# A decoder block on one core: wider runs for two scratch tensors in HBM

## The chip, the cores and the metric

One core of one Trainium2 chip. The metric is the device time of the whole program in microseconds (us), median of several executions; lower is better. Before: 1619.41 us, median of 3 runs (1616.14 to 1623.07).

## What is computed

One layer on 512 tokens of width 1024: a state-space mixer and an attention mixer side by side, then a layer of 16384 small experts. Only the expert layer matters here. Cut to that:

```python
def _peer(h, w_query, keys1, keys2, u_tab, v_tab):      # u_tab, v_tab: 16384 x 1024
    ...
    expert = e1 * PEER_NKEYS + e2                        # 8 heads x 16 experts of each token
    g = jax.nn.softmax(top_s.astype(jnp.float32), axis=-1)
    act = jax.nn.gelu(jnp.einsum('thkd,td->thk', u_tab[expert], ht))
    return jnp.einsum('thk,thkd->td', g * act, v_tab[expert])
```

## The kernel before

The expert layer takes two thirds of the time. For 384 of the 512 tokens it is computed densely: the 16384 experts are 128 blocks of 128 (a block is one value of `e1`, its 128 partitions the values of `e2`). The other 128 tokens are served by gathers: POOL issues 128 indirect DMAs of 512 KB from `peer_u` and 128 from `peer_v` into an eight-deep ring, and DVE uses the rows (L1737, L1745).

**Activation stage**, blocks b = 0 to 127. SP loads 512 KB of `peer_uT` into `u_raw` (L1440, four buffers). ACT copies it to the rounded `uth` (L1554), POOL computes the rest `utl` (L1535), PE makes 24 matmuls of 384 columns (L1649 to L1651), ACT applies gelu into `acts` (L1566). After each odd block SP stores two blocks of activations, 384 KB, to `act_scr` (`store_acts`, L1444). In blocks 57 to 112 PE also builds the routing weights of each token as a 128x128 matrix from one-hot matrices (L1664, L1665), ACT evacuates them four tokens at a time to `stage` (L1590), and SP stores each chunk of 32 tokens, 2 MB, to `g_scr` (L1449). `g_scr` is laid out as partition, chunk of 32 tokens (12 of them), block (128), token in the chunk (32).

**Value stage**, blocks n = 0 to 127, in pairs p = n // 2. SP loads activations of a pair (`load_a`, 384 KB, L1466, two buffers), value rows (`load_v`, 512 KB a block, L1454, four buffers) and routing weights of four blocks (`load_g`, 768 KB, L1457, two buffers). DVE multiplies activations and weights to `w_f` (L1853), ACT rounds it to `wh` and the values to `vh` (L1554), DVE makes the rest `wl` (L1858), POOL the rest `vl` (L1541), PE makes 18 matmuls of 512 columns (L1672 to L1674). `wh`, `wl`, `vh` and `vl` have four buffers each, so that DVE and POOL may be up to four blocks ahead of PE.

All direct DMAs of both stages are issued by SP in the order that the code of that engine writes out, and go into one queue (q1). The gathers of POOL go into another (q0). Both are served by the same 16 DMA engines. In the value stage SP's order for pair p is: wait until `w_done` is 2p - 2, [routing weights of the next four blocks, for odd p], activations of pair p, values of block 2p (after `vl_done`), values of block 2p + 1. Some single loads are put in between (pairs 16, 20, 24, and `x1b` at 28, 32, 36, 40).

The first loads of the value stage are issued in the last blocks of the activation stage: values 0 and 1, then routing weights 0, activations 0, values 2, activations 1, values 3, routing weights 1.

Of the kernel before, what the change touches and what calls it, by code (L numbers as in the profile page):

```python
# [5 lines left out]
F32 = mybir.dt.float32  # L6
# [6 lines left out]
ALU = mybir.AluOpType  # L13
AXX = mybir.AxisListType.X

P = 128
# [14 lines left out]
PH, PKEYS, PTOP, PHALF = 8, 128, 16, 128  # L31
# [22 lines left out]
class Plan:  # L54


    def __init__(self, nc):
        self.nc = nc
        self.u_scr = nc.dram_tensor("u_scr", (S5W, T), F32).ap()
        self.mod_scr = nc.dram_tensor("mod_scr", (2, 4, 512), F32).ap()  # L60
        self.y_scr = nc.dram_tensor("y_scr", (S5W, T), F32).ap()
        self.x1_scr = nc.dram_tensor("x1_scr", (T, D), F32).ap()
        self.g_scr = nc.dram_tensor("g_scr", (P, TD // CHK, PKEYS, CHK), F32).ap()
        self.act_scr = nc.dram_tensor("act_scr", (PKEYS, P, TD), F32).ap()
        self.dve_steps = Steps(self.sem("dve_stepped"))
        self.pool_steps = Steps(self.sem("pool_stepped"))
        self.base = (nc.sbuf_base + 63) // 64 * 64
# [1111 lines left out]
NBLK = PKEYS  # L1179
SP = P  # L1180
TD = T - SP
DT = TD // P
CHK = 32
HOTS = 4
BATCH = 16
GROUPS4 = TD // HOTS
NBATCH = TD // BATCH
# [6 lines left out]
def place_peer(k):  # L1194
# [45 lines left out]
    k.wTl = k.sb("wTl", [P, P], 200.5, F16)  # L1240
    k.stage = k.sb("stage", [P, 2, PKEYS, CHK], 110)


def place_values(k):

    k.vh = k.sb("vh", [P, 4, D], 110, F32R)
    k.vl = k.sb("vl", [P, 4, D], 126, F32R)
    k.v_raw = k.sb("v_raw", [P, 4, D], 78)
    k.wl = [k.sb(f"wl{i}", [P, TD], 182 + 1.5 * i, F32R) for i in range(4)]
    k.wh = [k.sb(f"wh{i}", [P, TD], at, F32R) for i, at in enumerate((94, 95.5, 188, 205))]  # L1250
    k.a_in = k.sb("a_in", [P, 2, 2, TD], 174)
    k.gate2 = k.sb("gate2", [P, D], 98)
    k.g_in = k.sb("g_in", [P, 2, TD // CHK, 4, CHK], 190)
    k.w_f = k.sb("w_f", [P, 2, TD], 202)

    k.y = k.sb("y", [P, TT, D], 6)
    k.ln2_g = k.sb("ln2_g", [P, D], 22)
    k.ln2_b = k.sb("ln2_b", [P, D], 26)
    k.stats2 = k.sb("stats2", [P, TT, 2, 6], 30)
    k.mv2 = k.sb("mv2", [P, TT, 2], 30.25)  # L1260
    k.rstd2 = k.sb("rstd2", [P, TT], 30.5)
    k.nmu2 = k.sb("nmu2", [P, TT], 30.625)
    k.x1b = k.sb("x1b", [P, TT, D], 38)
# [127 lines left out]
def experts(nc, io, k, ps, out):  # L1391
# [10 lines left out]
    act_stored = [k.sem(f"s_act_stored{i}") for i in range(2)]  # L1402
    g_stored = [k.sem(f"s_g_stored{i}") for i in range(2)]
    a_loaded = [k.sem(f"s_a_in{i}") for i in range(2)]
    g_loaded = [k.sem(f"s_g_in{i}") for i in range(2)]
    v_in = [k.sem(f"s_v_in{i}") for i in range(4)]
    row_in = [k.sem(f"s_row_in{i}") for i in range(RING)]
    mm = nc.tensor.matmul
    NCH = TD // CHK
    PER_CH = CHK // HOTS  # L1410
    PER_BATCH = BATCH // HOTS

# [23 lines left out]
    @k.block.sync  # L1436
    def _(sp):
        def load_u(b):
            sp.wait_ge(k.utl_done, b - 3)
            sp.dma_start(k.u_raw[:, b % 4], io["peer_uT"][b]).then_inc(k.s_u[b % 4], 16)  # L1440

        def store_acts(p):
            sp.wait_ge(k.gelu_done, 2 * p + 2)
            sp.dma_start(k.act_scr[2 * p:2 * p + 2].rearrange("e p t -> p e t"),  # L1444
                         k.acts[:, 2 * (p % 2):2 * (p % 2) + 2]).then_inc(act_stored[p % 2], 16)

        def store_g(ch):
            sp.wait_ge(k.g_evac, PER_CH * (ch + 1))
            sp.dma_start(k.g_scr[:, ch], k.stage[:, ch % 2]).then_inc(g_stored[ch % 2], 16)  # L1449

        def load_v(n):
            if n >= 4:
                sp.wait_ge(k.vl_done, n - 3)
            sp.dma_start(k.v_raw[:, n % 4], io["peer_v"][0][n * P:(n + 1) * P, :]).then_inc(v_in[n % 4], 16)  # L1454

        def load_g(q):
            sp.dma_start(k.g_in[:, q % 2].rearrange("p c e t -> p c (e t)"),  # L1457
                         k.g_scr[:, :, 4 * q:4 * q + 4].rearrange("p c e t -> p c (e t)")).then_inc(g_loaded[q % 2], 16)

        def load_a(p):  # L1460
            if p >= 2:
                sp.wait_ge(k.w_done, 2 * p - 2)
                if p % 2 and p < NBLK // 2 - 1:
                    load_g((p + 1) // 2)
            sp.wait_ge(act_stored[p % 2], 16 * (p // 2 + 1))
            sp.dma_start(k.a_in[:, p % 2], k.act_scr[2 * p:2 * p + 2].rearrange("e p t -> p e t")).then_inc(a_loaded[p % 2], 16)  # L1466

        for b in range(NBLK):
            if b + 4 < NBLK:
                load_u(b + 4)  # L1470
            if b % 2 and b < NBLK - 1:
                store_acts(b // 2)
            if b in STORE_AT:
                store_g(STORE_AT[b])
            if b == NBLK - 6:
                sp.wait_ge(k.g_out, GROUPS4)
                load_v(0)
                load_v(1)
            if b == NBLK - 5:
                for c in range(2):  # L1480
                    sp.wait_ge(g_stored[c], 16 * (NCH // 2))
                load_g(0)
                load_a(0)
                load_v(2)
                load_a(1)
                load_v(3)
                load_g(1)

        def load_vector(dst, src, sem):
            sp.dma_start(dst[:, :], bass.AP(src.tensor, src.offset, [[0, P], [1, D]])).then_inc(sem, 16)  # L1490

        for p in range(2, NBLK // 2):
            load_a(p)
            load_v(2 * p)
            load_v(2 * p + 1)
            if p == 2:
                store_acts(NBLK // 2 - 1)
            elif p == 16:
                load_vector(k.gate2, k.mod_scr[1, 2:4].rearrange("g n -> (g n)"), s_gate2)
            elif p == 20:  # L1500
                sp.wait_ge(k.act_out, NBLK)
                load_vector(k.ln2_g, io["ln2_g"], k.s_ln2)
            elif p == 24:
                load_vector(k.ln2_b, io["ln2_b"], k.s_ln2)
                sp.wait_ge(k.s_x1out, 16 * TT)
            elif p >= 28 and p % 4 == 0 and p < 28 + 4 * TT:
                t = p // 4 - 7
                sp.dma_start(k.x1b[:, t], k.x1_scr[t * P:(t + 1) * P, :]).then_inc(k.s_x1b, 16)

        for t in range(TT - 1):  # L1510
            sp.wait_ge(k.y_ready, t + 1)
            sp.dma_start(out[0, t * P:(t + 1) * P, :], k.y[:, t, :]).then_inc(k.s_out, 16)
        for half in range(2):
            cols = slice(half * 512, (half + 1) * 512)
            sp.wait_ge(k.y_last, half + 1)
            sp.dma_start(out[0, T - P:T, cols], k.y[:, TT - 1, cols]).then_inc(k.s_out, 16)
        sp.wait_ge(k.s_out, 16 * (TT + 1))
# [35 lines left out]
    def _(act):  # L1553
# [31 lines left out]
        def evacuate_g(n):  # L1585
            ch, at = n // PER_CH, n % PER_CH * HOTS
            if n % PER_CH == 0 and ch >= 2:
                act.wait_ge(g_stored[ch % 2], 16 * (ch // 2))
            act.wait_ge(k.g_out, n + 1)
            nc.scalar.activation(k.stage[:, ch % 2, :, at:at + HOTS],  # L1590
                                 ps[:, 4 + n % 2].rearrange("p (t e) -> p e t", t=HOTS), ACT.Copy, scale=1.0 / W_UP).then_inc(k.g_evac, 1)

# [127 lines left out]
    def _(dve):  # L1720
# [122 lines left out]
            tt(k.hot1l[m % 2][:, :, :], eq, wl, ALU.mult).then_inc(k.hot_ready, 1)  # L1843

        def weight(n):
            p, q = n // 2, n // 4
            if n % 2 == 0:
                dve.wait_ge(a_loaded[p % 2], 16 * (p // 2 + 1))
            if n % 4 == 0:
                dve.wait_ge(g_loaded[q % 2], 16 * (q // 2 + 1))  # L1850
            if n >= 2:
                dve.wait_ge(k.wl_done, n - 1)
            tt(k.w_f[:, n % 2].rearrange("p (c t) -> p c t", t=CHK), k.a_in[:, p % 2, n % 2].rearrange("p (c t) -> p c t", t=CHK),  # L1853
               k.g_in[:, q % 2, :, n % 4], ALU.mult).then_inc(k.w_done, 1)

        def split_w_low(n):
            dve.wait_ge(k.wh_done, n + 1)
# [37 lines left out]
        for t in range(DT):  # L1895
            at = slice(t * P, (t + 1) * P)
# [5 lines left out]
        use_rows(SLOTS - done["rows"])  # L1902

        weight(0)
        for n in range(1, NBLK):
            weight(n)
# [120 lines left out]
```

## Time and profile before

| what | us |
|---|---|
| median of 3 runs | 1619.41 |
| the profiled execution, its own time | 1620.23 |
| its span | 1618.4 |
| PE busy | 1525.7 (94% of the span) |
| DVE busy | 1269.3 (78%) |
| POOL busy | 996.8 (62%) |
| ACT busy | 688.2 (43%) |
| direct DMAs (q1), share of the 16 engines | 53.2% |
| gathers (q0), share of the 16 engines | 22.6% |

Busy PE time is modelled from the starts of pipelined matmuls; short gaps between two of them can be hidden in it. A share of the DMA engines is the sum of the times that the packets took over 16 times the stretch, and can be above 100%, since packets overlap. A packet here is one contiguous run. "Idle before" names what ended the wait of an engine.

### The profile page before, as it was taken

Reading aid. Unit: us, or ns where it says so; the run is one execution under the profiler, and the core shown is the slowest. Engines: PE = TensorE matmul, PEld = TensorE weight load, DVE = VectorE, ACT = ScalarE, POOL = GpSimd, SP = SyncE. Lnnn points to the kernel's source line nnn. Section 1 sums busy time; section 2 is a strip of 40 time slices with the busy share of each in tenths; the row PEclk is TensorE's granted clock in tenths of the full one; section 3 lists DMA queues with packets and bytes.
Section 4 is the critical chain, followed back from the end, with each engine's and each line's share of the span. In section 5 each row is a group of like instructions: output and inputs, shape, how many; then the busy total and the mean of one; then the engine's idle time right before and its main releaser. Section 6 shows DMA issues by size and latency. Waiting matters only on the chain.

```text
span 1618.4 us, 21748 instructions
## 1 busy us (share of the span) xinstructions
PE 1525.7 (94%) x7951; PEld 1268.7 (78%) x7951; DVE 1269.3 (78%) x2000; ACT 688.2 (43%) x1273; POOL 996.8 (62%) x608
## 2 busy tenths in 40 slices
PE   6996997978999999999999999999999999999996
PEld 2344575437889999999999998998888888788875
DVE  6768741283889999969887897549989888999997
ACT  2030464204233433358877876344333333333332
POOL 3511000023326777776766887788978888889875
PEclk9997999989999999999999999999999999999998
DMA  9974205412306787778898999999999999999971
GB/s 367 327 216 53 30 1 186 165 52 87 122 27 206 258 277 278 269 266 326 335 361 345 355 376 346 417 333 378 376 379 362 376 376 382 383 370 383 372 267 65
DMA packets 217302, 438.91 MB, mean 271 GB/s; under 512 B 37220, under 2 KB 129892, under 8 KB 215404
## 3 DMA queue, kind: packets, MB, share of 16 engines
q1 hardware_dynamic: 179612, 302.44, 53.2%
q0 software_dynamic: 36864, 134.23, 22.6%
q8 instruction: 63, 1.03, 0.3%
q10 hardware_dynamic: 720, 0.85, 0.2%
q14 instruction: 43, 0.35, 0.1%
HBM read 379.66 MB, written 56.64 MB: 270 GB/s over the span
## 4 chain that ended last, share of the span: by engine, by line
PE 26%; DMA 21%; issue 8%; DVE 8%; ACT 7%; POOL 4%; SPq 2%; POOLq 0%; ACTq 0%; DVEq 0%
DMA u_raw<-in_peer_uT 9%; DMA a_in<-act_scr 7%; DMA v_raw<-in_peer_v 6%; PE ps L1649 5%; PE ps L1650 5%; PE ps L1651 5%; ACT hot1h L1582 3%; POOL vl L1541 3%; DVE ps L1745 2%; PE ps L1327 2%; PE ps L1328 2%; PE ps L1329 2%; DVE w_f L1853 2%; DVE wl L1858 1%; ACT stage L1590 1%
## 5 line engine op out<-in xcount | busy, mean ns | idle before, releaser
L1535 POOL TENSOR_TENSOR utl<-u_raw,uth 128x1024 fp32r<-128x1024 f32 x128 | 307.2, 2401 | 150.3 <-ACT uth L1554 148.9
L1649 PE MATMUL ps<-h2h,uth 128*128 128x384 f32 x1024 | 348.2, 340 | 3.1 <-POOL utl L1535 3.1
L1541 POOL TENSOR_TENSOR vl<-v_raw,vh 128x1024 fp32r<-128x1024 f32 x128 | 311.5, 2435 | 52.4 <-ACT vh L1554 50.4
L1651 PE MATMUL ps<-h2h,utl 128*128 128x384 f32 x1024 | 343.2, 335 | 0.0
L1650 PE MATMUL ps<-h2l,uth 128*128 128x384 f32 x1024 | 342.9, 335 | 0.0
L1672 PE MATMUL ps<-vh,wh 128*128 128x512 f32 x768 | 300.0, 391 | 2.8 <-DVE wl L1858 2.6
L1673 PE MATMUL ps<-vl,wh 128*128 128x512 f32 x768 | 298.9, 389 | 0.0
L1674 PE MATMUL ps<-vh,wl 128*128 128x512 f32 x768 | 298.9, 389 | 0.0
L1853 DVE TENSOR_TENSOR w_f<-a_in,g_in 128x384 f32<-128x384 f32 x128 | 213.0, 1664 | 51.7 <-DMA a_in<-act_scr 50.7
L1554 ACT ACTIVATE vh<-v_raw 128x1024 fp32r<-128x1024 f32 x128 | 135.3, 1057 | 205.9 <-DMA v_raw<-in_peer_v 165.6
L1649 PEld LDWEIGHTS ps<-h2h,uth 128*128 128x128 f32 x1024 | 192.9, 188 | 3.8 <-POOL utl L1535 3.0
L1650 PEld LDWEIGHTS ps<-h2l,uth 128*128 128x128 f32 x1024 | 193.1, 189 | 0.0
L1651 PEld LDWEIGHTS ps<-h2h,utl 128*128 128x128 f32 x1024 | 192.7, 188 | 0.0
L1737 DVE CUSTOM_DVE_ANT_0 junk<-ring,ps 128x1024 bf16<-128x1024 f32 x128 | 150.4, 1216 | 32.6 <-DMA ring<-in_peer_u,row_at 32.3
L1672 PEld LDWEIGHTS ps<-vh,wh 128*128 128x128 f32 x768 | 144.1, 188 | 36.6 <-DVE wl L1858 6.3
L1674 PEld LDWEIGHTS ps<-vh,wl 128*128 128x128 f32 x768 | 144.2, 188 | 29.9
L1673 PEld LDWEIGHTS ps<-vl,wh 128*128 128x128 f32 x768 | 144.2, 188 | 29.6
L1745 DVE SCALAR_TENSOR_TENSOR ps<-ring,w_sp,ps 128x1024 f32<-128x1024 f32 x127 | 162.4, 1279 | 1.7
L1554 ACT ACTIVATE uth<-u_raw 128x1024 fp32r<-128x1024 f32 x128 | 134.9, 1056 | 66.5 <-DMA u_raw<-in_peer_uT 56.9
L1529 POOL DMA_INDIRECT ring<-in_peer_u,row_at x128 | 136.6, 1067 | 23.3 <-issue 12.0
L1529 POOL DMA_INDIRECT ring<-in_peer_v,row_at x128 | 137.1, 1071 | 22.4 <-issue 20.4
L1040 POOL TENSOR_TENSOR x<-x,ln_b 128x1024 f32<-128x1024 f32 x4 | 9.4, 2346 | 198.3 <-DVE x L1115 198.3
(357 smaller groups left out, 2338.5 us busy)
## 6 DMA issues: line engine op xcount, KB each, us to landing
u_raw<-in_peer_uT SPq DMA_DIRECT2D x128, 512.0 KB
v_raw<-in_peer_v SPq DMA_DIRECT2D x128, 512.0 KB
w_ada<-in_w_ada SPq DMA_DIRECT2D x12, 2048.0 KB, 14.6
act_scr<-acts SPq DMA_DIRECT2D x64, 384.0 KB
g_scr<-stage SPq DMA_DIRECT2D x12, 2048.0 KB
g_in<-g_scr SPq DMA_DIRECT2D x32, 768.0 KB
a_in<-act_scr SPq DMA_DIRECT2D x64, 384.0 KB
w_q<-in_peer_w_query SPq DMA_DIRECT2D x8, 1024.0 KB, 5.4
```

The lines of the kernel that those rows point to most:

```text
L1529: nc.gpsimd.indirect_dma_start(k.ring[j % RING][:, :], None, table, bass.IndirectOffsetOnAxis(ap=k.row_at[:, slot:slot + 1], axis=0)).then ...
L1535: tt(k.utl[b % 3][:, :, :].rearrange(f3), k.u_raw[:, b % 4].rearrange(f3), k.uth[b % 3][:, :, :].bitcast(F32).rearrange(f3), ALU.subtract) ...
L1541: tt(k.vl[:, n % 4], k.v_raw[:, n % 4], k.vh[:, n % 4].bitcast(F32), ALU.subtract).then_inc(k.vl_done, 1)
L1554: copy = lambda dst, src: nc.scalar.activation(dst, src, ACT.Copy)
L1649: mm(o, hi, k.h2h[:, kt, SP:T], start=(kt == 0), stop=False)
L1650: mm(o, hi, k.h2l[:, kt, SP:T], start=False, stop=False)
L1651: ins = mm(o, lo, k.h2h[:, kt, SP:T], start=False, stop=(kt == DK - 1))
L1672: mm(o, hi, k.vh[:, n % 4, cols], start=(n == 0), stop=False)
L1673: mm(o, hi, k.vl[:, n % 4, cols], start=False, stop=False)
L1674: return mm(o, lo, k.vh[:, n % 4, cols], start=False, stop=(n == NBLK - 1))
L1745: ins = v.scalar_tensor_tensor(y_sp, row, w, y_sp, ALU.mult, ALU.add)
L1853: tt(k.w_f[:, n % 2].rearrange("p (c t) -> p c t", t=CHK), k.a_in[:, p % 2, n % 2].rearrange("p (c t) -> p c t", t=CHK), k.g_in[:, q % 2, ...
```

## The change

`act_scr` gets the layout (pair of blocks, partition, block of the pair, token), so that both its store and its load have one run of 3072 bytes for each partition, in place of two of 1536. `load_g` reads eight blocks at a time, in runs of 1024 bytes in place of 512; each of its two buffers is 12 KB of a partition in place of 6 KB, the second one in the place of the activation stage's `uth` and `utl`. Routing weights 2, 3, ... are then loaded at pairs 5, 9, 13, ... (before: at 3, 5, 7, ...), and routing weights 1 at the end of pair 2, behind the last store of activations, in place of the last blocks of the activation stage.

```diff
-        self.act_scr = nc.dram_tensor("act_scr", (PKEYS, P, TD), F32).ap()
+        self.act_scr = nc.dram_tensor("act_scr", (PKEYS // 2, P, 2, TD), F32).ap()
+GROWS = 8
-    k.g_in = k.sb("g_in", [P, 2, TD // CHK, 4, CHK], 190)
+    k.g_in = [k.sb(f"g_in{i}", [P, TD // CHK, GROWS, CHK], at) for i, at in enumerate((190, 54))]
         def store_acts(p):
             sp.wait_ge(k.gelu_done, 2 * p + 2)
-            sp.dma_start(k.act_scr[2 * p:2 * p + 2].rearrange("e p t -> p e t"),
-                         k.acts[:, 2 * (p % 2):2 * (p % 2) + 2]).then_inc(act_stored[p % 2], 16)
+            sp.dma_start(k.act_scr[p], k.acts[:, 2 * (p % 2):2 * (p % 2) + 2]).then_inc(act_stored[p % 2], 16)
         def load_g(q):
-            sp.dma_start(k.g_in[:, q % 2].rearrange("p c e t -> p c (e t)"),
-                         k.g_scr[:, :, 4 * q:4 * q + 4].rearrange("p c e t -> p c (e t)")).then_inc(g_loaded[q % 2], 16)
+            sp.dma_start(k.g_in[q % 2][:, :, :, :].rearrange("p c e t -> p c (e t)"),
+                         k.g_scr[:, :, GROWS * q:GROWS * (q + 1)].rearrange("p c e t -> p c (e t)")).then_inc(g_loaded[q % 2], 16)
         def load_a(p):
             if p >= 2:
                 sp.wait_ge(k.w_done, 2 * p - 2)
-                if p % 2 and p < NBLK // 2 - 1:
-                    load_g((p + 1) // 2)
+                if p % (GROWS // 2) == 1 and p > GROWS // 2 and (p - 1) // (GROWS // 2) + 1 < NBLK // GROWS:
+                    load_g((p - 1) // (GROWS // 2) + 1)
             sp.wait_ge(act_stored[p % 2], 16 * (p // 2 + 1))
-            sp.dma_start(k.a_in[:, p % 2], k.act_scr[2 * p:2 * p + 2].rearrange("e p t -> p e t")).then_inc(a_loaded[p % 2], 16)
+            sp.dma_start(k.a_in[:, p % 2], k.act_scr[p]).then_inc(a_loaded[p % 2], 16)
...
                 load_v(3)
-                load_g(1)
...
             if p == 2:
                 store_acts(NBLK // 2 - 1)
+                load_g(1)
...
         def weight(n):
-            p, q = n // 2, n // 4
+            p, q = n // 2, n // GROWS
...
-            if n % 4 == 0:
+            if n % GROWS == 0:
                 dve.wait_ge(g_loaded[q % 2], 16 * (q // 2 + 1))
...
-               k.g_in[:, q % 2, :, n % 4], ALU.mult).then_inc(k.w_done, 1)
+               k.g_in[q % 2][:, :, n % GROWS], ALU.mult).then_inc(k.w_done, 1)
```

## Rows read from the trace of the kernel before

**Rows 1.** The page: busy us, share of the span and instructions of each engine.

```profile
PE 1525.7 (94%) x7951; PEld 1268.7 (78%) x7951; DVE 1269.3 (78%) x2000; ACT 688.2 (43%) x1273; POOL 996.8 (62%) x608
```

**Rows 2.** Windows by stage: busy us (count) of PE, PEld, DVE, ACT, POOL; clock, DMA share, GB/s.

```profile
480.00:700.00 220.00, 220.00 (x1271) 220.00 (x1270) 210.97 (x600) 86.55 (x117) 162.27 (x89) 1.00 0.73 252
700.00:1050.00 350.00, 336.22 (x2418) 325.19 (x2417) 275.44 (x261) 254.56 (x618) 264.31 (x161) 1.00 0.93 353
1078.00:1550.00 472.00, 469.25 (x2062) 385.71 (x2061) 428.79 (x353) 173.18 (x230) 414.11 (x243) 1.00 1.02 373
1550.00:1606.00 56.00, 55.97 (x247) 45.86 (x245) 50.36 (x54) 21.44 (x29) 34.69 (x15) 1.00 0.42 148
```

**Rows 3.** Line L1672: durations in ns, first and last start in us.

```profile
L1672 PE MATMUL ps<-vh,wh x768: 387/389/504, 1078.2 to 1605.3; 128*128 128x512 f32 x192
```

**Rows 4.** Timeline of PE: two L1672 starts twelve triples apart, and around 1415 us.

```profile
1079.62 0.39 PE L1672 MATMUL ps<-vh,wh 128*128 128x512 f32 x1
...
1087.79 0.39 PE L1672 MATMUL ps<-vh,wh 128*128 128x512 f32 x1
...
1414.80 0.39 PE L1674 MATMUL ps<-vh,wl 128*128 128x512 f32 x1
1416.27 0.50 PE L1672 MATMUL ps<-vh,wh 128*128 128x512 f32 x1 [1.08 <-DVE wl L1858]
```

**Rows 5.** Chain that ended last, 1395 to 1420 us: start, us, what.

```profile
1396.89 0.53 SPq L1457
...
1397.46 4.11 SPq L1466
...
1401.61 10.16 DMA v_raw<-in_peer_v
```

**Rows 6.** Timeline of DVE, early and around 1410 us.

```profile
1072.26 2.56 DVE L1858 TENSOR_TENSOR wl<-w_f,wh 128x384 fp32r<-128x384 f32 x1
1074.92 2.57 DVE L1853 TENSOR_TENSOR w_f<-a_in,g_in 128x384 f32<-128x384 f32 x1
...
1109.49 0.55 DVE L1858 TENSOR_TENSOR wl<-w_f,wh 128x384 fp32r<-128x384 f32 x1
...
1409.71 0.56 DVE L1853 TENSOR_TENSOR w_f<-a_in,g_in 128x384 f32<-128x384 f32 x1 [2.57 <-DMA a_in<-act_scr]
1410.19 0.55 DVE L1858 TENSOR_TENSOR wl<-w_f,wh 128x384 fp32r<-128x384 f32 x1
...
1415.67 0.55 DVE L1858 TENSOR_TENSOR wl<-w_f,wh 128x384 fp32r<-128x384 f32 x1
```

**Rows 7.** DMA queues, 1085 to 1086 us: packets, MB, share of the 16 engines.

```profile
q1 hardware_dynamic: 656, 0.34, 114.0%
```

**Rows 8.** DMA queues, 493 to 494 us: 84 packets of 4096 bytes, 14 semaphore writes.

```profile
DMA packets 98, 0.34 MB, mean 344 GB/s; under 512 B 14, under 2 KB 14, under 8 KB 98
...
q1 hardware_dynamic: 98, 0.34, 84.3%
```

**Rows 9.** DMA queues and issues, 1100 to 1550 us.

```profile
q1 hardware_dynamic: 74436, 103.48, 65.1%
...
v_raw<-in_peer_v SPq DMA_DIRECT2D x109, 512.0 KB
a_in<-act_scr SPq DMA_DIRECT2D x54, 384.0 KB
g_in<-g_scr SPq DMA_DIRECT2D x27, 768.0 KB
```

**Rows 10.** Waits, 700 to 1050 us: total us, times, longest.

```profile
ACT uth L1554 <- DMA u_raw<-in_peer_uT: 55.2, 17, 6.6
...
PE ps L1664 <- ACT stage L1590: 11.4, 10, 2.0
```

**Rows 11.** Chain that ended last, from 1017 us: the longest wait for `u_raw`, the first activations.

```profile
1017.65 17.67 DMA u_raw<-in_peer_uT
...
1063.41 7.67 DMA a_in<-act_scr
```

## The prediction

> **What bounds the kernel now.** I read the page first, then windows by stage, then the value stage's PE instructions, then what DVE and the queues do there.
>
> The page shows PE busy 94% of the span, far above the other engines [rows 1]. The windows say where the DMA engines are full beside it [rows 2]. From 480 to 700 us PE is busy without a gap and the DMA engines are 73% busy. From 700 to 1050 us PE misses 13.8 us (350 - 336.2), DMA 93%. From 1078 to 1550 us PE misses 2.8 us by this count while DMA stands at 102%. After 1550 us there are no gathers left and DMA falls to 42%.
>
> The value stage has to be read finer than by busy time, which hides gaps. Its 768 L1672 matmuls start from 1078.2 to 1605.3 us [rows 3], that is 527.1 us for 767 steps of three matmuls. Where PE runs undisturbed, twelve such steps take 1087.79 - 1079.62 = 8.17 us [rows 4], 0.681 each. 767 x 0.681 = 522.2 us. So **PE loses only about 5 us in the whole value stage**: it sets the pace, at 6 x 0.681 = 4.085 us for each block, and nothing that makes loads faster can give back more than 5 us there.
>
> Those 5 us have a pattern. Block 9 is to start on PE at 1078.2 + 9 x 4.085 = 1115.0 us, and its `wl` (the tenth L1858) ends at 1110.04 [rows 6]: DVE is 4.9 us ahead. Block 81's `wl` ends at 1410.74, within 0.1 us of its start on PE. Then `w_f` has waited 2.57 us for activations, the next `wl` ends at 1416.22 [rows 6], and PE starts at 1416.27 where 1414.80 + 0.23 was due: 1.2 us lost [rows 4]. The chain goes back from there to the queue of SP: weights load at 1396.89, the activations' issue held for 4.11 us behind it, then a value load that takes 10.16 us to land where 512 KB alone need 1.3 us (below) [rows 5]. The transfers wait for each other. The lead of DVE and POOL on PE is eaten slowly, and stalls come when it is gone.
>
> **The change, part by part.** Price of a packet first. In 1085 to 1086 us 656 packets move 0.34 MB, some 512 bytes each, at 1.14 x 16 x 1000 / 656 = 27.8 ns [rows 7]. In 493 to 494 us, 84 packets of 4096 bytes take (0.843 x 16000 - 14 x 9) / 84 = 159 ns, with the 14 tiny ones at the 9 ns that a packet without bytes has by the line below [rows 8]. A straight line through both gives 0.0366 ns a byte and 9.1 ns a packet: 46.5 ns for 1024 bytes, 65.3 for 1536, 121.5 for 3072. No row shows 1024 or 3072. Bounds: at best they cost by the byte what 4096 do (40 and 119), at worst two of the small ones (55.6 and 131). I take the line, since sizes between two measured ones should lie between. It checks: in 1100 to 1550 us, 27 weight loads of 1536 packets, 54 activation loads of 256 and 109 value loads and four of `x1b` of 128 come to 4355 engine-us, against 0.651 x 450 x 16 = 4690 shown for q1 [rows 9], 8% more, as packets that meet others take longer.
>
> *Weights, 512 to 1024 bytes.* 32 loads of 1536 packets become 16 of 1536. Each pair of packets saves 2 x 27.8 - 46.5 = 9.1 ns; 24,576 pairs / 16 engines = 14.0 us of DMA time (bounds 0 and 24). *Activations read, 1536 to 3072.* 8192 pairs x 9.1 / 16 = 4.7 us (0 to 6). *Activations stored,* the same 4.7 us, over the activation stage. SP issues 16 DMAs less, at 0.53 us [rows 5], hidden behind its waits for DVE's `w_done`.
>
> What this means for eight blocks of the value stage, DMA time: before, weights 2 x 2.67, activations 4 x 1.04, values 8 x 1.27, gathers (one each 0.875 block) 9.14 x 1.27: 31.3 us, against PE's 32.7. After: weights 4.46, activations 3.89: 30.1 us. The slack goes from 1.4 to 2.6 us in eight blocks. Rows say that the nominal slack of 1.4 was not enough to hold DVE's lead. With nearly twice of it the lead should recover between the dips, and DVE (428.8 of 472 us busy) and POOL (414.1) still fit under PE [rows 2]. I take 3.5 of the 5 us back (bounds 0 and 5).
>
> *What it adds.* A weight load now is 1.5 MB ahead of the activations of a pair, at 4.5 us in place of 2.7 if alone: 1.8 us later, up to 3.6 when a gather shares the engines, at every fourth pair in place of every second. DVE must pay that from its lead. If the lead stays above 2 us it costs nothing; at a lead of zero each of the 14 loads in the saturated stretch would cost 1.8 us. Queued behind the wait are the two value loads of the pair, so POOL's `vl` is late by the same.
>
> *The start of the stage.* Weights 0 are doubled too, and activations 0 behind them took 7.67 us [rows 11]; they come 1.8 us later. Block 0's `wl` ended at 1074.8 [rows 6], 3.4 us before PE's 1078.2. Covered, by 1.6 us. Weights 1 move behind the last store of activations and are needed for block 8 only; they put the activations of pair 3 back by 1.8 us, whose lead there is some 5 us [rows 6]. Nothing.
>
> *Activation stage.* PE's waits there are for ACT's evacuation (11.4 us), and ACT is late because it waits in order for `u_raw` (55.2 us, 17 times) [rows 10]; the longest, 17.67 us [rows 11], lies behind a 2 MB weights store. Of the store of activations that is also ahead in the queue, 128 x 9.1 / 16 = 0.07 us goes. Seventeen waits and one or two such stores ahead of each: 1 to 2 us of waiting, of which PE sees less. I take 0.5 us (bounds 0 and 2.4, which is the saving of all 33 stores from 700 us on). From 480 to 700 us PE has no gap, and nothing can come of it.
>
> The Trainium skill (DMA: Bandwidth & Descriptors, Specifications) puts the smallest transfer at line rate at 512 bytes. By that rule the weights already go at full rate and their part saves nothing. This trace disagrees: 18.4 bytes a ns at 512 against 25.8 at 4096. The same page (Why small descriptors are slow) gives a fixed 3 cycles beside one for each 32 bytes; at 19 against 35 cycles of its 850 MHz fabric that is an estimate of 5.4 us saved on the weights where rows give 14.0.
>
> **Sum.** Against the profiled execution's own 1620.2 us: 3.5 in the value stage and 0.5 in the activation stage make 1616.2. The median of the runs is 0.8 us under that execution: **1615.5 us**.
>
> **Rivals.**
>
> *Nothing moves* (chance 0.22). The lead is eaten by something else, DVE and POOL blocking each other (`w_f` takes 0.56 to 2.57 us [rows 6]), or the small packets' cost is hidden as that rule of 512 bytes has it. For it: DVE is 91% busy in the stage. Against: chains around the stalls end in transfers. Time: 1618 to 1620.5.
>
> *The burst decides, and it is slower* (0.13). Place: the activations behind a 1.5 MB weights load. The lead late in the stage is 0.1 to 2 us, under the 1.8 to 3.6 us of the burst. If no lead is rebuilt, 14 bursts x 1.8 = 25 us; with half of it rebuilt some 12, less the 4 gained. It decides from the point where the lead at pairs 5, 9, 13, ... is under 1.8 us. For it: rows 5 and 6 show exactly this wait. Against: DVE gets 8 blocks between bursts and 1.2 us more slack in them. Time: 1622 to 1640.
>
> *More than the value stage* (0.12). The activation stage's 13.8 us of gaps close by half because shorter stores let `u_raw` come earlier and the row gathers move. Against: 0.07 us a store. Time: 1606 to 1611.
>
> The forecast itself, 1613 to 1618, has 0.53.
>
> **How the numbers follow.** Half a per cent, 8.1 us, is about what a measurement of this kernel can tell from no change. Faster by more needs more than the value stage can give: most of the third rival and a little luck, 0.10. Slower by more is the upper half of the burst: 0.08. The rest, 0.82, is within. The range for 8 in 10 leaves out the far ends of both: 1609 to 1624.
>
> **What the profile would show.** Right: q1's packets fall by 24,576 + 16,384 in all; 32 weight loads become 16, about 4.5 us each; the L1672 starts span 523 to 525 us; waits of `w_f` for activations are fewer but longer ones stand at every fourth pair; PE's gaps before 1050 us as before. Wrong: that span above 527 us with PE waiting for `wl` just behind a weights load (the burst), or unchanged with DVE's lead as small as now though DMA share fell (DVE and POOL), or PE's starts in the activation stage closing up by several us.

## The result: 1.6% slower, and the profile after

The changed kernel takes 1648.95 us (median of 4 runs, 1637.11 to 1655.19) against 1619.48 for the kernel before: ratio 1.016, 95% interval 1.011 to 1.021. I had predicted 1615.5 with a range to 1624.0, and gave "slower by more than half a per cent" 0.08. The rival that came true is the second of the three, that the burst decides; it had 0.13, and the measured time lies above its range (1622 to 1640) too. Of the executions further down four stood far above the others of their kernel (1947.6, 2217.3, 1637.2 and 1640.9 us), and the ratios leave them out.

The profiled execution took 1637.11 us, the fastest of the four; its profile shows the mechanism, not the full size. The page of the changed kernel, busy times and all DMA packets [rows 1]:

```profile
PE 1531.7 (94%) x7951; PEld 1268.7 (78%) x7951; DVE 1261.0 (77%) x2000; ACT 684.2 (42%) x1273; POOL 993.4 (61%) x608
...
q1 hardware_dynamic: 138396, 302.44, 52.5%
```

No engine has more instructions than before, and q1 has 41,216 packets less (138,396 against 179,612; forecast 40,960, the other 256 fit the 16 semaphore writes of each of 16 DMAs less). But PE is busy 6 us more with the same 7951 matmuls; the reason is below. Its windows by stage, with the same columns and bounds as [rows 2]:

```profile
480.00:700.00 220.00, 220.00 (x1272) 220.00 (x1270) 209.34 (x600) 86.50 (x117) 162.53 (x89) 1.00 0.73 252
700.00:1050.00 350.00, 338.24 (x2438) 327.23 (x2438) 272.93 (x261) 256.37 (x621) 267.01 (x163) 1.00 0.93 355
1078.00:1550.00 472.00, 457.92 (x1977) 372.36 (x1976) 409.11 (x340) 162.84 (x220) 396.88 (x235) 0.99 0.97 361
```

The activation stage is as before or a little better (338.2 us busy against 336.2). The value stage lost: PE misses 14.1 us where it missed 2.8, and the DMA share fell from 102% to 97%. Less traffic, less time in it, and later all the same. The line L1672 of the changed kernel, instruction and reasons of its waits [rows 3]:

```profile
L1672 PE MATMUL ps<-vh,wh x768: 387/389/690, 1074.0 to 1622.3; 128*128 128x512 f32 x192
...
  DVE wl L1858: 40.2, 41
```

The value stage now spans 548.3 us where the undisturbed pace would need 522.2: 26 us lost in place of 5, from a start 4.2 us earlier. (The 40.2 us count the same gaps twice, once for the weight load and once for the matmul.) Who waited for whom in 1090 to 1550 us:

```profile
ACT wh L1554 <- DVE w_f L1853: 174.0, 77, 5.4
ACT vh L1554 <- DMA v_raw<-in_peer_v: 126.9, 43, 8.9
POOL vl L1541 <- ACT vh L1554: 51.6, 14, 6.2
DVE w_f L1853 <- DMA a_in<-act_scr: 51.5, 14, 6.3
```

Fourteen waits of DVE for activations and fourteen of POOL for values (through ACT), 3.7 us each on average, with 13 weight loads in the stretch. The same stretch of the kernel before:

```profile
DVE w_f L1853 <- DMA a_in<-act_scr: 33.9, 18, 4.4
POOL vl L1541 <- ACT vh L1554: 33.7, 17, 4.8
```

So before there were more such waits, of 1.9 to 2.0 us each. One of the longest of the changed kernel, in its timelines of SP, DVE, POOL and PE:

```profile
1371.92 0.52 SPq L1457 DMA_DIRECT2D g_in<-g_scr  x1
1372.49 2.03 SPq L1466 DMA_DIRECT2D a_in<-act_scr  x1
1374.57 2.41 SPq L1454 DMA_DIRECT2D v_raw<-in_peer_v  x2
```

```profile
1388.04 0.56 DVE L1853 TENSOR_TENSOR w_f<-a_in,g_in 128x384 f32<-128x384 f32 x1 [5.88 <-DMA a_in<-act_scr]
1388.51 0.55 DVE L1858 TENSOR_TENSOR wl<-w_f,wh 128x384 fp32r<-128x384 f32 x1
```

```profile
1372.74 2.41 POOL L1541 TENSOR_TENSOR vl<-v_raw,vh 128x1024 fp32r<-128x1024 f32 x1
1375.30 1.10 POOL L1529 DMA_INDIRECT ring<-in_peer_v,row_at  x1 [0.16 <-issue]
1376.71 0.93 POOL L1529 DMA_INDIRECT ring<-in_peer_v,row_at  x1 [0.30 <-issue]
1377.66 2.40 POOL L1541 TENSOR_TENSOR vl<-v_raw,vh 128x1024 fp32r<-128x1024 f32 x1
...
1391.10 2.41 POOL L1541 TENSOR_TENSOR vl<-v_raw,vh 128x1024 fp32r<-128x1024 f32 x1 [6.25 <-ACT vh L1554]
...
1394.77 2.41 POOL L1541 TENSOR_TENSOR vl<-v_raw,vh 128x1024 fp32r<-128x1024 f32 x1
...
1398.45 2.43 POOL L1541 TENSOR_TENSOR vl<-v_raw,vh 128x1024 fp32r<-128x1024 f32 x1
```

```profile
1386.11 0.39 PE L1674 MATMUL ps<-vh,wl 128*128 128x512 f32 x1
1389.12 0.50 PE L1672 MATMUL ps<-vh,wh 128*128 128x512 f32 x1 [2.62 <-DVE wl L1858]
```

The weights load is issued at 1371.92. The activations behind it land at 1388.0, 15.5 us after their issue; the values behind those are the piece of the chain that ended last:

```profile
1374.57 15.37 DMA v_raw<-in_peer_v
```

DVE stands idle for 5.88 us, POOL for 6.25. Then see how fast POOL catches up: one `vl` each 3.68 us (1391.10, 1394.77, 1398.45), with a gather between two of them, against PE's 4.085 for a block. But there are eight gathers to seven blocks, so that about every seventh block holds two, and that one takes 4.92 us (1372.74 to 1377.66). Seven blocks are 6 x 3.68 + 4.92 = 27.0 us against PE's 28.6: **POOL regains some 1.8 us in the eight blocks from one burst to the next, and a burst makes it wait 3.7 us on average. The rest, some 1.9 us for each of 14 waits or 26 us in all, is PE's**, and 26 us is what PE lost. (PE waits for DVE's `wl`, and the sum goes by POOL. DVE's waits add up to the same, 51.5 us, and its `w_f` start as far apart, 3.67 us from 1373.48 to 1377.15; which of the two engines sets their common pace isn't tested.)

The kernel before closes by the same sum. Some 107 blocks fall between 1090 and 1550 us, so POOL can regain about 24 us there (an estimate, 107 / 8 x 1.8). Its waits were 33.7 us: the 10 us beyond that ate the lead, and cost PE its 5 us when the lead was gone. With waits of 51.6 us there is no more to regain, and what is added goes to PE.

Not all of PE's 26 us is waiting. After three of the long waits its granted clock fell to half, 1.2 GHz, for 3.4 us each (1247.8, 1319.5 and 1425.3 us). The first, after a wait of 2.02 us, in the windows and in PE's timeline:

```profile
1247.80:1251.20 3.40, 3.40 (x10) 2.62 (x9) 2.49 (x3) 2.46 (x4) 1.94 (x1) 0.50 1.04 411
```

```profile
1248.40 0.63 PE L1673 MATMUL ps<-vl,wh 128*128 128x512 f32 x1
1248.83 0.63 PE L1674 MATMUL ps<-vh,wl 128*128 128x512 f32 x1
```

Matmuls then start 0.43 us apart in place of 0.23. Half of 3.4 us is lost each time, 5.1 us of the 26 in all. (While PE is slow the engines behind it regain lead, so without the dips some of this could have come as waits; no run separates it.) The clock stood at 1.00 through the whole value stage of the kernel before. This is where most of PE's 6 us more of busy time comes from.

### The profile page after: what moved, and what is told of

It is laid out like the page before. It is cut to its first block, busy times and chain, and to the rows that moved or that the text cites. A ratio compares the mean times of both kernels' runs of the same rounds, so it can differ in the third digit from the quotient of the medians.

```text
span 1635.3 us, 21748 instructions
## 1 busy us (share of the span) xinstructions
PE 1531.7 (94%) x7951; PEld 1268.7 (78%) x7951; DVE 1261.0 (77%) x2000; ACT 684.2 (42%) x1273; POOL 993.4 (61%) x608
## 3 DMA queue, kind: packets, MB, share of 16 engines
q1 hardware_dynamic: 138396, 302.44, 52.5%
## 4 chain that ended last, share of the span: by engine, by line
PE 27%; DMA 20%; issue 9%; DVE 8%; ACT 7%; POOL 4%; SPq 2%; POOLq 0%; ACTq 0%; DVEq 0%
DMA v_raw<-in_peer_v 9%; DMA u_raw<-in_peer_uT 9%; PE ps L1649 6%; PE ps L1650 6%; PE ps L1651 6%; ACT hot1h L1582 3%; DVE ps L1745 2%; DMA a_in<-act_scr 2%; POOL vl L1541 2%; PE ps L1328 2%; PE ps L1330 2%; PE ps L1329 2%; DVE wl L1858 2%; DVE w_f L1853 2%; ACT stage L1590 1%
## 5 line engine op out<-in xcount | busy, mean ns | idle before, releaser
L1672 PE MATMUL ps<-vh,wh 128*128 128x512 f32 x768 | 303.5, 395 | 15.6 <-DVE wl L1858 15.2
L1853 DVE TENSOR_TENSOR w_f<-a_in,g_in 128x384 f32<-128x384 f32 x128 | 209.0, 1633 | 70.5 <-DMA a_in<-act_scr 69.7
L1672 PEld LDWEIGHTS ps<-vh,wh 128*128 128x128 f32 x768 | 145.1, 189 | 54.7 <-DVE wl L1858 24.9
L1554 ACT ACTIVATE wh<-w_f 128x384 fp32r<-128x384 f32 x128 | 66.5, 520 | 193.0 <-DVE w_f L1853 193.0
```

Source lines behind the costliest of these rows:

```text
L1554: copy = lambda dst, src: nc.scalar.activation(dst, src, ACT.Copy)
L1672: mm(o, hi, k.vh[:, n % 4, cols], start=(n == 0), stop=False)
```

## Experiments

All ratios are against the kernel before on the same chip, with 95% intervals. "Gaps" is the span of the starts of the first value matmul (L1672 or its like) in the profiled execution, less 522.2 us.

### Which half of the change it is

Pair layout of the activations alone (the `act_scr` hunks of the diff), and eight rows at a time alone (the rest of it).

> The pair layout of the activations alone; routing weights as before, four blocks at a time. Burst theory (the 1.5 MB load ahead of the activations makes them late, and DVE and POOL regain too little of their lead before the next one): the layout is innocent, 0 to 5 us faster than before. Rival, layout theory (runs of 3072 bytes in the store or the load cost time, or block others for longer): most of the change's +17 to +35 us is here. A second rival, that the packets' size never mattered: within 1 us of before.

> Eight rows of weights at a time alone; activations in the old layout. Burst theory: 20 to 35 us slower than before, a little worse than the full change, with PE stalling behind each weights load. Layout theory: within 5 us of before.

Measured: the layout alone 0.999 (0.997 to 1.001), gaps none (522.0 us) in its profiled execution, which was the fastest of ten (1613.9 us) and so doesn't show that the layout removes the 5 us of before. Eight rows alone 1.019 (1.016 to 1.021), gaps 42 us. The layout is innocent; on its own it can't be told from before, and beside the eight rows it takes little or nothing away (1.019 against 1.016, intervals overlap).

### Run size or burst

The changed kernel with two loads of four rows in 512-byte runs, back to back; and with two loads of 768 KB in 1024-byte runs, at separate pairs.

```diff
+            for h in range(2):            # 512-byte runs, same burst
+                at = slice(4 * h, 4 * h + 4)
+                sp.dma_start(k.g_in[q % 2][:, :, at]..., k.g_scr[:, :, GROWS * q + 4 * h:GROWS * q + 4 * h + 4]...)
```

> The changed kernel with runs of 512 bytes again: the weights of eight blocks are loaded by two DMAs of four blocks, back to back at the same place. Burst theory: as slow as the change or slower, +20 to +40 us over before, since 5.3 us of DMA time stand ahead of the activations in place of 4.5. Rival, that runs of 1024 bytes from rows 16 KB apart are what is slow: back to within 5 us of before.

```diff
+        def load_g_part(q, parts):        # 1024-byte runs, half the burst
+            for h in parts:
+                at = slice(6 * h, 6 * h + 6)          # chunks of 32 tokens
+                sp.dma_start(k.g_in[q % 2][:, at]..., k.g_scr[:, at, GROWS * q:GROWS * (q + 1)]...)
...
+                q, r = (p - 1) // 4 + 1, (p - 1) % 4
+                if p >= 3 and r % 2 == 0 and q < NBLK // GROWS:
+                    load_g_part(q, [r // 2])
```

> The changed kernel with each weights load cut in two DMAs of 768 KB by tokens, one at every second pair as before, still in runs of 1024 bytes. Burst theory: 2 to 6 us faster than before (1612 to 1618), since both the packets and the burst are small. Rival, that 1024-byte runs or the place of the buffers are slow: as slow as the change.

Measured: small runs in a burst 1.029 (1.027 to 1.032), the slowest of all, 47 us over before where I had expected 20 to 40, gaps 50 us; wide runs in halves 0.997 (0.995 to 0.999). Against the change the halves have the same bytes, the same runs, the same buffers and the same index of eight rows on DVE. What differs is the size of one load, and with it that the second half comes two pairs later; 1.6% slower becomes 0.3% faster. The value stage of the halved variant, its windows row and its L1678 (the same matmul):

```profile
1078.00:1550.00 472.00, 472.00 (x2084) 390.81 (x2083) 452.05 (x362) 172.14 (x234) 418.62 (x244) 1.00 1.00 380
```

```profile
L1678 PE MATMUL ps<-vh,wh x768: 387/389/499, 1077.4 to 1599.3; 128*128 128x512 f32 x192
```

521.9 us: no gap is left.

### Place of the burst

The 1.5 MB load issued behind the activations but ahead of the pair's values, or behind both.

```diff
         def load_a(p):
...
             sp.dma_start(k.a_in[:, p % 2], k.act_scr[p])...
+            if p % 4 == 1 and p > 4 and (p - 1) // 4 + 1 < NBLK // GROWS:
+                load_g((p - 1) // 4 + 1)              # burst_mid; burst_last: after load_v(2 * p + 1)
```

> The changed kernel with the same 1.5 MB weights loads, each issued behind the activations and the two value loads of its pair in place of ahead of them; nothing needs it before seven blocks later. Theory that what costs is the place (the burst ahead of transfers that are needed at once): most of the 30 us comes back, 1612 to 1625. Rival, that a burst costs wherever it stands, since the next pair's activations queue behind it: 1640 to 1655 again. I hold 1625 to 1640 for likeliest: the values of the pair are spared, the next pair's activations are not quite.

> The changed kernel with each 1.5 MB weights load between the activations of its pair and the values of its pair. The changed kernel's trace shows both landing late behind a burst (activations 15.5 us after their issue, values 15.4), and the values' chain ending last. If the values are the ones that bind: 1640 to 1655, no better than the change. If the activations bind: near the variant with the burst behind both, 1625 to 1632.

Measured: behind both 1.004 (1.002 to 1.006), in the range I held likeliest, gaps 10.5 us; ahead of the values 1.013 (1.010 to 1.016), 1642.1 us, in the range of "the values bind", gaps 25 us. With the load ahead of the values DVE waits for activations only once in 1090 to 1550 us (8.6 us), while POOL waits for values 51.2 us in 13 times, as in the changed kernel (51.6 in 14). So values that are late cost nearly as much as values and activations that are late together. The rows of both, behind both first:

```profile
L1672 PE MATMUL ps<-vh,wh x768: 387/389/504, 1080.2 to 1612.9; 128*128 128x512 f32 x192
```

```profile
L1672 PE MATMUL ps<-vh,wh x768: 387/389/632, 1078.6 to 1626.1; 128*128 128x512 f32 x192
```

### Smaller still, and at another place

Four loads of 384 KB, one at each pair; two of 768 KB behind the pair's values; and the kernel before with the pair layout and its 768 KB loads cut in two by tokens, so 384 KB in runs of 512 bytes.

> The weights of eight blocks in four DMAs of 384 KB, one at every pair, runs of 1024 bytes. Burst theory: no worse than two of 768 KB (0.997 of before), perhaps 1 us faster; the value stage has no gaps left to give. Rival, that DMAs' count or SP's issues matter: slower than two by 2 us or more. The last quarter of each group is issued only at the pair that needs it, just ahead of its activations.

> Two DMAs of 768 KB with runs of 1024 bytes, each behind the values of its pair. Both theories: the value stage is at PE's pace already, so the same as two ahead of the activations, within 2 us. Slower by 5 us or more would say that the place behind the values is worse than the place ahead.

> The kernel before with the pair layout of the activations and each 768 KB weights load cut in two by tokens, one at each pair: loads of 384 KB in runs of 512 bytes. Against the four-part variant (384 KB at each pair in runs of 1024 bytes, 0.997 of before) only the size of the runs differs. If runs of 1024 bytes are worth something at this load: slower than 0.997, up to before or a little over. If the size of the load alone decides: 0.997 again, 1614 to 1617.

Measured: 0.997 (0.995 to 0.999), 0.998 (0.995 to 1.001) and 0.998 (0.996 to 0.999). No two of them can be told apart, and none has gaps above 1 us. Against the four-part variant the last one has the same bytes, the same place and size of each load but for the first blocks, and runs of weights half as long (its buffers hold four blocks in place of eight). The longer runs of the activations alone gave 0.999 above. **The longer runs, which the change was about, are worth nothing measurable here.** Once PE has no gaps, DMA time that is saved has nowhere to go.

### Gathers left out

No gathers of value rows; POOL fills a small tile and DVE computes on old rows in the ring, so that the output of the first 128 tokens is not the layer's.

```diff
+            if j >= SLOTS:
+                ...
+                nc.gpsimd.memset(k.junk[1][:, :], 0.0).then_inc(s_fill, 1)
+                return
```

> The changed kernel, 1.5 MB bursts in their place, with the 128 gathers of value rows left out (so the output of the first 128 tokens is not the reference's): POOL fills a small tile in their place, DVE computes on what stands in the ring. If the burst is stretched by the gathers that share the engines with it: it lands in about 6 us in place of 11.6, the activations behind it in about 6 to 7, PE has no gaps in the value stage beyond 1 us, 1605 to 1612. Rival, that DVE's and POOL's own pace keeps the lead down whatever the queue does: gaps of 10 us and more remain and the time stays above 1630.

Measured: 0.998 (0.996 to 1.000), 1617.5 us; the profiled execution 1611.2. The issues of the changed kernel in 1100 to 1550 us, the last column the median us from issue to landing, and then the same without gathers:

```profile
v_raw<-in_peer_v SPq DMA_DIRECT2D x104, 512.0 KB, 8.6
a_in<-act_scr SPq DMA_DIRECT2D x52, 384.0 KB, 8.8
g_in<-g_scr SPq DMA_DIRECT2D x13, 1536.0 KB, 11.9
```

```profile
v_raw<-in_peer_v SPq DMA_DIRECT2D x111, 512.0 KB, 4.6
a_in<-act_scr SPq DMA_DIRECT2D x55, 384.0 KB, 4.1
g_in<-g_scr SPq DMA_DIRECT2D x13, 1536.0 KB, 9.3
```

```profile
L1679 PE MATMUL ps<-vh,wh x768: 387/389/500, 1074.1 to 1596.4; 128*128 128x512 f32 x192
```

The gaps are gone (522.3 us), with the same bursts. The burst itself still takes 9.3 us, where I had expected 6; the loads around it land in 4.6 and 4.1 us in place of 8.6 and 8.8. The time is 5 us above what I expected, though the mechanism is as expected: of the variants with halved and quartered loads, which have no gaps either, most executions take 1611 to 1622 us. This run removes DMA load and also frees POOL from generating the gathers, so it doesn't say which of the two gave the room. Its trace shows how much room there is: in 1078 to 1560 us DVE waits for activations only 11.1 us in 11 times (51.5 in 14 in the changed kernel), and ACT waits for a buffer that PE holds,

```profile
ACT vh L1561 <- PE ps L1681: 298.5, 116, 2.6
```

so that the lead stands at the most that the four buffers allow.

### A threshold or a proportion

The two-part load cut nine chunks to three (1.15 MB and 0.38 MB).

```diff
-                at = slice(6 * h, 6 * h + 6)
+                at = (slice(0, 9), slice(9, 12))[h]
```

> The two-part load cut unevenly: nine chunks of tokens (1.15 MB) at pairs 5, 9, 13 and three (0.38 MB) at pairs 7, 11, 15. Theory of a threshold (a burst costs what it takes from DVE's and POOL's lead beyond what they win back at 0.41 us a block, 3.3 us in eight blocks): between, 1620 to 1634, nearer to the lower end. Rival, cost in proportion to the size of the largest load from zero: half way, 1632 or so, and the even cut could not have been free.

Measured: 1.004 (1.002 to 1.006), 1629.5 us, gaps 14 us. Between, as the threshold has it, but in the upper half of its interval where I had said the lower end: the 3.3 us in eight blocks that the expectation gives left out the blocks with two gathers, and 1.8 is nearer. POOL's waits say the same: 39.9 us in 14 times in 1090 to 1550 us, 2.9 each, less 1.8 regained makes 1.1 x 14 = 15 us, where gaps are 14. With nothing lost at 0.77 MB, 14 at 1.15 and 26 at 1.5 there is a threshold at 0.77 MB or above it; these three points don't place it. A proportion from zero would not leave the even cut at none. But 1629 is also near the 1632 of the rival's half way, so it is the pair with the even cut that decides, not this run alone.

### Order on DVE

At blocks 8k + 2, `wl` of the block before is made first, then the product that waits.

```diff
+            if n % 8 == 2:
+                split_w_low(n - 1)
+                weight(n)
```

> The changed kernel with DVE's order turned at blocks 8k + 2: wl of the block before first, then the product that waits for the activations behind the burst. Theory that the late landing sets the stall: PE's gap moves by a block and stays the same size, 1640 to 1655. Rival, that the order on DVE (wl of a block ready long before, queued behind the wait) makes the stall: 10 to 25 us come back.

Measured: 1.018 (1.014 to 1.023), nothing gained. Its timeline of DVE around one burst:

```profile
1248.07 2.11 DVE L1858 TENSOR_TENSOR wl<-w_f,wh 128x384 fp32r<-128x384 f32 x1
1254.63 0.56 DVE L1853 TENSOR_TENSOR w_f<-a_in,g_in 128x384 f32<-128x384 f32 x1 [4.45 <-DMA a_in<-act_scr]
```

The `wl` that used to sit behind the wait now ends 4.5 us before it; PE then stalls one block later, in one piece. The landing sets the stall, not DVE's order.

## Why the prediction was wrong, step by step

**What bounds the kernel** was right. PE's pace of 4.085 us a block, about 5 us lost in the stage, nothing to win beyond: four variants with smaller weight loads brought the gaps to none or next to it, and gained 0.2 to 0.3%, 3 to 5 us.

**The price of a packet** was right where it can be checked. In 1388 to 1390 us of the run without gathers only 1024-byte packets move:

```profile
q1 hardware_dynamic: 723, 0.74, 105.7%
```

1.057 x 2 x 16000 / 723 = 46.8 ns, where the line gave 46.5. By the Trainium skill's rule of full rate from 512 bytes (DMA: Bandwidth & Descriptors, Specifications) there was nothing to save, and this trace disagrees: two runs of 512 bytes took 2 x 27.8 = 55.6 ns [rows 7]. The whole saving was smaller than computed. Over the value stage q1 took 62.5% of 528 us before and 58.4% of 548.7 us after, 330.0 and 320.4 us: 9.6 us less, where weights and activations read were to give up to 18.7. The prices are from stretches in which q1 ran alone; that packets which meet others cost more would fit, and isn't shown here. What was saved was worth nothing.

**The step that failed** is "with nearly twice of it the lead should recover between the dips". I worked the recovery out of the DMA engines' slack, 1.2 us more in eight blocks. Recovery isn't theirs to give: the lead is made by POOL and DVE, at their own pace, and POOL's, with its gathers, is 3.68 us for most blocks and 4.92 for about every seventh. That gives 1.8 us in eight blocks before as after, and the waits of the kernel before (33.7 us in 460) already took more than that. So there was no reserve: the waits grew to 51.6 us, and PE's loss from 5 to 26. In my sum the burst stood at nothing, because the lead was to stay above it. [rows 2] had POOL busy 414.1 of 472 us, and I used it only to say that POOL fits under PE. The slack itself was worked out with prices of undisturbed packets, while [rows 2] showed a DMA share of 102%.

**The price of a burst** was about right on average and too low for the longest. I put the activations 1.8 us later, 3.6 at most. The average wait grew from 2.0 us to 3.7. But DVE's wait at the burst shown is 5.88 us and POOL's 6.25, against 2.57 at the one of before [rows 6], and the half clock after such waits was in no term. Two things were missing for the long ones. The gathers' queue is served beside this one, and shares the engines with the burst and with what lies behind it. In 1374 to 1384 us of the changed kernel:

```profile
q1 hardware_dynamic: 1624, 1.94, 57.2%
q0 software_dynamic: 394, 1.44, 39.6%
```

And the two value loads of the pair are late as well; I named them and charged nothing, though the run with the burst between activations and values shows that they alone cost 1.3%.

**My sum for the rival** (25 us if nothing is rebuilt, 12 if half) came out near the 26 us of gaps by luck: it charged 1.8 us for each of 14 bursts and rebuilt nothing, where 3.7 were taken and some 1.8 rebuilt. What was wrong in the weights was its chance: rows 5 and 6 already showed a 768 KB load costing PE 1.2 us at a lead of 0.1, and a load of twice the size with the same small lead should have been the likeliest case.

**The start of the stage and the activation stage** were about right: PE's first value matmul is not later (1074.0 against 1078.2 us, from the one profiled execution of each) and the gaps from 700 to 1050 us changed by 2 us.

In the profiled execution the sum is then complete: 21 us more of gaps, less the start 4.2 us earlier, is 16.9, the difference between 1637.1 and 1620.2 us. The median is 29 us over before. Still open: why the four runs of the changed kernel spread over 18 us, where the other kernels with loads above 1 MB spread over 2 to 13. Only the fastest was profiled.

## What to carry to other kernels

A transfer that isn't urgent, ahead of urgent ones in one queue, is priced by the waits that it causes in the engines behind it against the lead that they regain until the next one. The lead is rebuilt at the rate by which those engines are faster than the bound, counted over a whole period with its costly blocks, and not by the DMA slack. Where, as here, PE is already the pace and transfers are only just hidden, cut prefetches small and spread them; DMA time saved by merging them bought nothing, and the merged burst cost 1.6%. The Trainium skill (DMA: Bandwidth & Descriptors, Rules for kernel authors) asks for 1 MiB or more in a DMA for bandwidth; here, where bandwidth wasn't what bound, 1.5 MB loads gave 1.016 and loads of 384 to 768 KB of the same bytes 0.997 to 0.998.

## What the runs showed of the hardware

Two queues with work share the engines neither by count of runs nor by bytes. In 1376 to 1377 us of the changed kernel q1 moves only 1024-byte runs of the burst, beside 4096-byte runs of the gathers:

```profile
q0 software_dynamic: 54, 0.20, 57.0%
q1 hardware_dynamic: 93, 0.10, 31.0%
```

The gathers have fewer runs (49, and 5 semaphore writes), but twice the bytes and nearly twice the time. A microsecond later it is 191 runs of q1 to 32 of q0, so this is one example and no rule. The Trainium skill (DMA: Bandwidth & Descriptors, Queues, rings and completion order) has each engine switch between its queues at packet boundaries, but its packet is typically some 9 to 17 descriptors and not the single run that is called a packet here; these counts neither confirm nor refute it. That the burst in 512-byte runs was the slowest kernel (1.029) may come from its twice as many runs beside the gathers or from its 0.8 us more of DMA time; no run here separates the two.

The granted clock of TensorE fell to 1.2 GHz for 3.4 us just after three waits of PE (2.02 us before 1247.8, 1.92 before 1319.5, 2.24 before 1425.3), and not after the longest (2.62 us before 1389.12).
